# Two inner norms: the first two projections start with nine unnormalised tiles, and the third moves ahead of the barrier

## The chip, the cores and the metric

One core of one Trainium2 chip runs the whole program. The metric is the device time of one execution in microseconds (us), the median of several runs. The engines are TensorE (PE in the rows, its weight loads PEld), VectorE (DVE), ScalarE (ACT), GpSimd (POOL) and SyncE (SP), which issues the stream of weights.

## What is computed

Three layers of a sequence model on x of 512 positions by 2048 features, then a last norm. Each layer is a norm, one wide projection, a mixer and an output projection that is added to the residual:

```python
def rmsnorm(x, g):
    y = xf * lax.rsqrt(jnp.mean(xf * xf, axis=-1, keepdims=True) + EPS)
    return (y * g)
def even_layer(x, ...):
    hn = rmsnorm(x, norm_g)
    proj = hn @ w_in          # q, k, v, u, z_a, z_b
    ...
    return x + jnp.concatenate([o_a, o_b], axis=-1) @ w_out
def odd_layer(x, ...):
    hn = rmsnorm(x, norm_g)
    proj = hn @ w_in          # q, k, v, z, f_logit
    log_f = jax.nn.log_sigmoid(f_logit + b_forget)
    ...
    return x + o @ w_out
```

The factor of the norm, rsqrt(mean of the squares), belongs to a position; the gain g belongs to a feature. The change is about the norms ahead of `even_layer` and of `odd_layer`, called inner norms here. In the even layer u goes through a state-space model (S5), whose matrices are made on the chip out of small parameters; in the odd layer the sum over positions of log_f is subtracted from the attention scores.

## The kernel before, in words

**Tiles and split.** Features lie on the 128 partitions, positions (512) in the free dimension, so x is KT = 16 tiles of 128x512 in `mix`. All float32 products are made of three rounded ones: a value is split in a rounded part (`hi`) and what is left (`lo`), and hi·hi, lo·hi and hi·lo are summed in PSUM. One output tile of 128 features (`gemm`, L274) is 16 k-tiles of three matmuls, 48 in all. `gemm_two` (L297) does two output tiles together, k-tile by k-tile, 96 matmuls, as the operands come out of a norm.

**The weights.** A tile of weights comes in two halves of 512 KB. SyncE loads a half into one of two `raw` places (L267) once the half two before it is split. ScalarE makes its hi part (`cast`, L486, instruction at L495), which waits for the load and for TensorE to be done with the place in `w_hi`; GpSimd then makes the lo part (L2527) and reports it in `split_done`, for which TensorE waits. I call these two a cast and a rest. Casts stand by hand in ScalarE's program, in `taken` (L497) for instance: cast, read-out of the finished output tile, cast. GpSimd does the rests in the order of the stream.

**Output projection and norm.** In `out_tensor` (L347) TensorE makes 16 output tiles; VectorE adds the residual into `mix` (L363) and sums the squares (`accumulate`, L334) that ScalarE makes (L383). Behind the last one `norm_tensor` (L329) sums over the partitions by one matmul with ones (L332), ScalarE takes the root (L442), VectorE the reciprocal (`rstd`, L455). Then for each of 16 tiles: VectorE multiplies by gain and `rstd` (L459) into one of four buffers, ScalarE rounds (L450), VectorE subtracts (L466), and TensorE multiplies that k-tile into the first two projections (`gemm_two`, L308 to L310).

**Barrier.** `meet` (L243) drains TensorE, ScalarE and VectorE and lets each on when all three are there. GpSimd and SyncE take no part. One stands behind the first two projections at both inner norms.

**Even layer behind its barrier.** The first two projections are tiles N_U and N_U + 1 of u. ScalarE issues five loads of parameters (`s5_scalar`, L2094) and takes u tile by tile (`take_u`, L2102). VectorE (`s5_vector`, L2244) waits for those loads and runs a chain of 89 small instructions, then `make` (L2344). TensorE (`s5_tensor`, L2006) does the tiles N_U + 2 to N_U + 5 of u, then `form(0, 0)` (L2047: L2054 and L2061), which needs what `make` left, then the tiles N_U + 6 and N_U + 7.

**Odd layer behind its barrier.** The first two projections are the forget gates (tile N_F) and q of head 0 (N_ODD = N_F + 1). ScalarE (`forget_scalar`, L1919) and VectorE (`forget_vector`, L1934) turn the gates into a running sum in a chain, the result goes to memory and comes back (`load_decay`, L1630), and only then ScalarE takes q, k, v and z of head 0 (`take`). TensorE goes on with tile N_ODD + 1 (k), which waits for the read-out of the gates, then N_ODD + 2 (v), which waits for the read-out of q:

```python
            for j in range(at.heads, 4):
                gemm(pe, at.n0 + j, (at.n0 + j) % 2, free=(evac_act, at.n0 + j - 1 - at.shift))
```

## Time and profile before

| | us |
|---|---|
| median of 3 runs | 3190.93 (3188.35 to 3192.02) |
| the profiled execution, its own time | 3191.25 |
| its span, first to last instruction | 3189.4 |
| TensorE busy | 2995.7 (94% of the span) |
| VectorE, ScalarE, GpSimd busy | 1166.8, 1175.7, 1206.6 (37, 37, 38%) |
| granted clock of TensorE, mean | 0.975 |

The profile gives each engine's instructions in order of time, with the idle time before them in brackets and what ended it. TensorE is busy nearly throughout, so what counts are the few stretches in which it is not. A matmul's duration in a row overlaps the next one's; the distance of two starts is what it costs.

### The profile page before, as it was taken

The numbers are of one execution on the slowest core, as the hardware profiler recorded it, in microseconds if no ns is written. First come the engines' busy times: TensorE is split into PE (matmuls) and PEld (weight loads), VectorE is DVE, ScalarE is ACT, GpSimd is POOL, SyncE is SP. The second block draws the span as 40 slices with busy tenths as digits, with TensorE's granted clock in tenths as the row PEclk, the third lists the DMA queues.
The fourth block names the chain that finished last, engine by engine and source line by source line (L and its number), as shares of the span: only waits on it lengthen the run. The fifth ranks groups of instructions, "written<-read, shape, count | busy, mean of one in ns | idle before, by whom it ended". The sixth has DMA issues, their size and how long they took to land.

```text
span 3189.4 us, 47246 instructions
## 1 busy us (share of the span) xinstructions
PE 2995.7 (94%) x18318; PEld 2388.6 (75%) x18318; DVE 1166.8 (37%) x1684; ACT 1175.7 (37%) x1577; POOL 1206.6 (38%) x549
## 2 busy tenths in 40 slices
PE   6999998989998988999989987998999999999998
PEld 5777776767776877777766766886888888888786
DVE  4555555333443128578814334114111111111112
ACT  4333333235565223333324443223333333333322
POOL 3222220433325434566623322443333333333542
PEclk9999999999999999999999998999999999999999
DMA  4211110322212442222223222442222223222232
GB/s 155 96 55 55 55 61 21 96 69 80 79 62 68 161 132 82 84 96 92 96 97 106 79 79 86 148 139 80 93 91 89 92 89 92 92 86 91 90 125 99
DMA packets 95331, 290.25 MB, mean 91 GB/s; under 512 B 10048, under 2 KB 14432, under 8 KB 94704
## 3 DMA queue, kind: packets, MB, share of 16 engines
q1 hardware_dynamic: 64512, 233.14, 23.2%
q10 hardware_dynamic: 30704, 55.43, 5.1%
q8 instruction: 90, 1.47, 0.2%
q14 instruction: 25, 0.20, 0.0%
HBM read 265.40 MB, written 23.13 MB: 90 GB/s over the span
## 4 chain that ended last, share of the span: by engine, by line
PE 61%; issue 20%; DVE 8%; POOL 5%; PEld 3%; ACT 2%; DMA 1%; PEldq 1%; DVEq 0%; ACTq 0%; POOLq 0%; SPq 0%
PE ps L291 14%; PE ps L293 14%; PE ps L292 14%; POOL w_lo L2527 5%; PE ps L688 3%; PE ps L690 3%; PE ps L689 3%; DVE arena L2375 1%; DVE arena L2405 1%; PE ps L1539 1%; PE ps L1557 1%; DVE mix L2368 1%; PE ps L740 1%; DVE arena L2412 1%; PE ps L1754 1%
## 5 line engine op out<-in xcount | busy, mean ns | idle before, releaser
L2527 POOL TENSOR_TENSOR w_lo<-raw,w_hi 128x1024 fp32r<-128x1024 f32 x442 | 1069.9, 2423 | 1897.6 <-ACT w_hi L495 1896.4
L291 PE MATMUL ps<-act_hi,w_hi 128*128 128x512 f32 x2240 | 890.8, 398 | 33.9 <-POOL w_lo L2527 19.4
L293 PE MATMUL ps<-act_lo,w_hi 128*128 128x512 f32 x2240 | 877.0, 392 | 0.0
L292 PE MATMUL ps<-act_hi,w_lo 128*128 128x512 f32 x2240 | 876.7, 391 | 0.0
L495 ACT ACTIVATE w_hi<-raw 128x1024 fp32r<-128x1024 f32 x442 | 466.6, 1056 | 712.1 <-PE ps L293 339.7
L291 PEld LDWEIGHTS ps<-act_hi,w_hi 128*128 128x128 f32 x2240 | 423.9, 189 | 133.6 <-issue 42.0
L292 PEld LDWEIGHTS ps<-act_hi,w_lo 128*128 128x128 f32 x2240 | 424.3, 189 | 90.6 <-issue 4.3
L293 PEld LDWEIGHTS ps<-act_lo,w_hi 128*128 128x128 f32 x2240 | 423.5, 189 | 89.4
L688 PE MATMUL ps<-act_hi,w_hi 128*128 128x512 f32 x768 | 309.1, 403 | 13.7 <-ACT arena L780 13.7
L689 PE MATMUL ps<-act_hi,w_lo 128*128 128x512 f32 x768 | 300.2, 391 | 0.0
L690 PE MATMUL ps<-act_lo,w_hi 128*128 128x512 f32 x768 | 300.0, 391 | 0.0
L363 DVE TENSOR_TENSOR mix<-ps,arena 128x512 f32 (+1 forms) x48 | 33.2, 692 | 436.9 <-PE ps L293 403.3
L688 PEld LDWEIGHTS ps<-act_hi,w_hi 128*128 128x128 f32 x768 | 144.7, 188 | 49.4 <-issue 19.7
L690 PEld LDWEIGHTS ps<-act_lo,w_hi 128*128 128x128 f32 x768 | 144.6, 188 | 31.3
L689 PEld LDWEIGHTS ps<-act_hi,w_lo 128*128 128x128 f32 x768 | 144.9, 189 | 29.1 <-issue 1.4
L992 PE MATMUL ps<-act_hi,w_hi 128*128 128x512 f32 x352 | 154.9, 440 | 0.0
L1664 DVE TENSOR_TENSOR ps<-ps,arena 128x128 f32<-128x128 f32 (+1 forms) x64 | 27.1, 492 | 347.5 <-PE ps L1539 347.5
L994 PE MATMUL ps<-act_lo,w_hi 128*128 128x512 f32 x352 | 138.9, 394 | 0.0
L993 PE MATMUL ps<-act_hi,w_lo 128*128 128x512 f32 x352 | 138.2, 393 | 0.0
L1680 DVE TENSOR_TENSOR mix<-ps,arena 128x512 f32 (+1 forms) x16 | 11.1, 692 | 287.9 <-PE ps L1557 287.9
L383 ACT ACTIVATE arena<-mix 128x512 f32 (+1 forms) x48 | 30.3, 630 | 224.9 <-DVE mix L363 224.9
L308 PE MATMUL ps<-act_hi,w_hi 128*128 128x512 f32 x192 | 80.6, 420 | 31.6 <-DVE act_lo L466 15.7
(374 smaller groups left out, 3469.9 us busy)
## 6 DMA issues: line engine op xcount, KB each, us to landing
raw<-stream SPq DMA_DIRECT2D x442, 512.0 KB, 3.5
arena<-residual ACTq DMA_DIRECT2D x48, 256.0 KB, 2.7
residual<-mix ACTq DMA_DIRECT2D x32, 256.0 KB, 2.1
mix<-x ACTq DMA_DIRECT2D x4, 1024.0 KB, 9.7
residual<-arena ACTq DMA_DIRECT2D x4, 1024.0 KB, 6.9
kept_qk<-mix ACTq DMA_DIRECT2D x16, 256.0 KB, 2.1
arena<-kept_qk ACTq DMA_DIRECT2D x16, 256.0 KB, 3.7
arena<-decays ACTq DMA_DIRECT2D x16, 256.0 KB, 3.1
```

What stands on the lines that cost most here:

```text
L291: pe.matmul(dst, w_hi[:, slot, j, :], act_hi[:, kt, :], start=first, stop=False)
L292: pe.matmul(dst, w_lo[:, slot, j, :], act_hi[:, kt, :], start=False, stop=False)
L293: mm = pe.matmul(dst, w_hi[:, slot, j, :], act_lo[:, kt, :], start=False, stop=last)
L308: a = pe.matmul(dst, w_hi[:, slot, j, :], act_hi[:, kt, :], start=kt == 0, stop=False)
L495: nc.scalar.activation(w_hi[:, s, :, :], src[:, s % 2, :, :], ACT.Copy).then_inc(cast_done, 1)
L688: self.pe.matmul(dst, w_hi[:, slot, j, :], act_hi[:, kt, :], start=kt == 0, stop=False)
L689: self.pe.matmul(dst, w_lo[:, slot, j, :], act_hi[:, kt, :], start=False, stop=False)
L690: mm = self.pe.matmul(dst, w_hi[:, slot, j, :], act_lo[:, kt, :], start=False, stop=kt == KT - 1)
L992: pe.matmul(dst, w_hi[:, slot, kt % HK, :], act_hi[:, kt, :], start=kt == 0, stop=False)
L993: pe.matmul(dst, w_lo[:, slot, kt % HK, :], act_hi[:, kt, :], start=False, stop=False)
L994: mm = pe.matmul(dst, w_hi[:, slot, kt % HK, :], act_lo[:, kt, :], start=False, stop=kt == KT - 1)
L2527: nc.gpsimd.tensor_tensor(w_lo[:, s, :, :], src[:, s % 2, :, :], w_hi[:, s, :, :].bitcast(F32), ALU.subtract).then_inc(split_done, 1)
```

## The change

The norm's matmul leaves the end of `out_tensor` in the first two layers. As VectorE puts tiles 0 to 8 into `mix`, ScalarE rounds mix times gain, without the norm's factor (`plain_round`), and VectorE subtracts (`plain_rest`), into 18 places of their own. `first_tensor` takes the place of `gemm_two`: the k-tiles 0 to 8 of the first two projections from those, into PSUM banks 2 and 3, with the norm's matmul behind the fourth k-tile; then the k-tiles 9 to 15 with the norm's factor, as before, into banks 4 and 5. `first_vector` multiplies banks 2 and 3 by `rstd` and adds 4 and 5. The norm makes its 16 tiles in the order 9 to 15, 0 to 8, and ahead of the barrier TensorE does the third projection (N_U + 2, N_F + 2) out of them in the order of k. Four casts move from behind the barrier to places behind the tiles 4, 10, 12 and 14 of the norm's order, in `norm_scalar`. The loops over the norm's tiles and five pairs of output tiles are written out. The last norm keeps its form.

```diff
-                        pe.wait_ge(act_ready[0], act_ready[1] + kt + 1)
+                        place = kt if len(act_ready) == 2 else act_ready[2].index(kt)
+                        pe.wait_ge(act_ready[0], act_ready[1] + place + 1)
...
+        PLAIN = 9
+        NORM_ORDER = [*range(PLAIN, KT), *range(PLAIN)]
+        plain_hi = [slots(arena_r, j) for j in range(PLAIN)]
+        plain_lo = [slots(arena_r, j) for j in (9, 10, 11, 12, 13, 14, 15, 20, 28)]
+        first_out = [slots(arena, 24), slots(arena, 25)]
+        plain_rounded = sem("plain_rounded")
+        plain_split = sem("plain_split")
+        first_scaled = sem("first_scaled")
+        first_summed = sem("first_summed")
+
+        def first_tensor(pe, n, norm):
+
+            def products(bank, tile, kt, hi, lo, first, last):
+                dst, slot, j = ps[:, bank, :], 2 * (tile % 2) + kt // HK, kt % HK
+                a = pe.matmul(dst, w_hi[:, slot, j, :], hi, start=first, stop=False)
+                pe.matmul(dst, w_lo[:, slot, j, :], hi, start=False, stop=False)
+                return a, pe.matmul(dst, w_hi[:, slot, j, :], lo, start=False, stop=last)
+
+            pe.wait_ge(split_done, n * 2 + 3)
+            for kt in range(PLAIN):
+                if kt == HK:
+                    pe.wait_ge(split_done, n * 2 + 4)
+                pe.wait_ge(plain_split, PLAIN * (norm - 1) + kt + 1)
+                for tile in (n, n + 1):
+                    _, mm = products(2 + tile - n, tile, kt, plain_hi[kt], plain_lo[kt], kt == 0, kt == PLAIN - 1)
+                    if tile == n and kt == HK - 1:
+                        mm.then_inc(pe_half, 1)
+                if kt == 3:
+                    norm_tensor(pe, norm)
+            for kt in range(PLAIN, KT):
+                pe.wait_ge(norm_lo, KT * norm + (kt - PLAIN) + 1)
+                for tile in (n, n + 1):
+                    a, mm = products(4 + tile - n, tile, kt, act_hi[:, kt, :], act_lo[:, kt, :], kt == PLAIN,
+                                     kt == KT - 1)
+                    if kt == KT - 1:
+                        mm.then_inc(pe_half, 1)
+                    if tile > n and kt == KT - 1:
+                        a.then_inc(pe_half, 1)
+            gemm(pe, n + 2, n % 2, free=(evac_dve, KT * norm), act_ready=(norm_lo, KT * norm, NORM_ORDER))
+
+        def plain_round(act, norm, ft):
+            nc.scalar.activation(plain_hi[ft], mix_tile(ft), ACT.Copy, scale=gain(norm, ft)).then_inc(plain_rounded, 1)
+
+        def plain_rest(dve, norm, ft):
+            dve.wait_ge(plain_rounded, PLAIN * (norm - 1) + ft + 1)
+            nc.vector.scalar_tensor_tensor(
+                out=plain_lo[ft], in0=mix_tile(ft), scalar=gain(norm, ft), in1=plain_hi[ft].bitcast(F32),
+                op0=ALU.mult, op1=ALU.subtract).then_inc(plain_split, 1)
+
+        def first_vector(dve, n, norm):
+            dve.wait_ge(pe_half, 2 * (n + 2))
+            for j in range(2):
+                nc.vector.tensor_tensor(first_out[j], ps[:, 2 + j, :], rstd, ALU.mult).then_inc(first_scaled, 1)
+            for j in range(2):
+                dve.wait_ge(first_scaled, 2 * (norm - 1) + j + 1)
+                nc.vector.tensor_tensor(first_out[j], first_out[j], ps[:, 4 + j, :],
+                                        ALU.add).then_inc(first_summed, 1)
...
-            norm_tensor(pe, layer + 1)
+            if layer == 2:
+                norm_tensor(pe, layer + 1)
...
+                    if layer < 2 and isinstance(ft, int) and 0 <= ft + j - 1 < PLAIN:
+                        plain_rest(dve, layer + 1, ft + j - 1)
...
+                if not last_layer and isinstance(ft, int) and ft + j < PLAIN:
+                    plain_round(act, layer + 1, ft + j)
...
-            with act.Fori(0, KT // 4) as four:
-                ft = four * 4
-                for j in range(4):
-                    act.wait_ge(norm_t, ft + (KT * (norm - 1) + j + 1))
-                    nc.scalar.activation(act_hi[:, bass.ds(ft + j, 1), :].rearrange("p a t -> p (a t)"),
-                                         norm_in[j], ACT.Copy).then_inc(norm_hi, 1)
+            n = (0, N_U, N_F)[norm]
+            weights = {3: 0, 9: 1, 11: 2, 13: 3}
+            for i, ft in enumerate(NORM_ORDER):
+                act.wait_ge(norm_t, KT * (norm - 1) + i + 1)
+                nc.scalar.activation(act_hi[:, ft, :], norm_in[i % 4], ACT.Copy).then_inc(norm_hi, 1)
+                if i in weights:
+                    cast(act, n * 2 + 4 + weights[i], (2 * n + weights[i]) % 4)
...
+            def rest(i):
+                ft = NORM_ORDER[i]
+                dve.wait_ge(norm_hi, KT * norm + i + 1)
+                nc.vector.tensor_tensor(act_lo[:, ft, :], norm_in[i % 4], act_hi[:, ft, :].bitcast(F32),
+                                        ALU.subtract).then_inc(norm_lo, 1)
+
+            if norm < 3:
+                for i, ft in enumerate(NORM_ORDER):
+                    if i >= 2:
+                        rest(i - 2)
+                    if i >= 4:
+                        dve.wait_ge(norm_lo, KT * norm + i - 3)
+                    scaled(ft, i % 4)
+                for i in (KT - 2, KT - 1):
+                    rest(i)
+                first_vector(dve, (0, N_U, N_F)[norm], norm)
...
-            for j in range(at.heads, 4):
+            for j in range(at.heads + 1, 4):
...
+                if isinstance(u, int) and u == 0 and j == 0:
+                    act.wait_ge(first_summed, 4)
+                    nc.scalar.activation(at_q_in, first_out[1], ACT.Copy, scale=at.scale).then_inc(evac_act, 1)
+                    return
...
-            pe.wait_ge(evac_dve, 2 * KT)
-            gemm_two(pe, N_F, norm_lo, 2 * KT)
+            first_tensor(pe, N_F, 2)
 
         def forget_scalar(act):
             act.dma_start(at_cmask, consts[:, C_ODD:C_ODD + P]).then_inc(at_const, 16)
-            par = N_F % 2
-            cast(act, N_F * 2 + 4, (2 * par) % 4)
-            act.wait_ge(pe_half, N_F * 2 + 2)
-            nc.scalar.activation(fg_t[0], ps[0:FR, par, :], ACT.Identity,
+            act.wait_ge(first_summed, 3)
+            nc.scalar.activation(fg_t[0], first_out[0][0:FR, :], ACT.Identity,
                                  bias=prm[0:FR, PRM_BF:PRM_BF + 1]).then_inc(evac_act, 1)
-            cast(act, N_F * 2 + 5, (2 * par + 1) % 4)
...
-            pe.wait_ge(evac_dve, KT)
-            gemm_two(pe, N_U, norm_lo, KT)
+            first_tensor(pe, N_U, 1)
...
-            for n in range(N_U + 2, N_U + S5_TILES):
+            for n in range(N_U + 3, N_U + S5_TILES):
...
+                if j < 2:
+                    act.wait_ge(first_summed, j + 1)
+                    nc.scalar.activation(mix_tile(8 + j), first_out[j], ACT.Copy).then_inc(evac_act, 1)
+                    return
```

The first place where the order changes is ScalarE's program at the first inner norm. Before: behind the norm's root, the roundings (L450, here four of a loop of four passes), the barrier (`met`), the five loads of parameters, the first cast, the first read-out of u.

```order
L442 ACTIVATE arena<-ps,eps 128x512 [waits res_stored]
...
L450 ACTIVATE act_hi<-arena 128x512
...
L2096 DMA arena<-consts 128x512 [waits met]
L2098 DMA arena<-s_b 128x512 x2
L2100 DMA arena<-s_c 128x512 x2
L495 ACTIVATE w_hi<-raw 128x1024 [waits pe_half,raw_loaded0]
L2104 ACTIVATE mix<-ps 128x512 [waits pe_half]
```

Now (L518 is the rounding, L565 the cast, L2175 the read-out of u's first two tiles):

```order
L518 ACTIVATE act_hi<-arena 128x512 [waits norm_t] x4
L565 ACTIVATE w_hi<-raw 128x1024 [waits pe_half,raw_loaded0]
L518 ACTIVATE act_hi<-arena 128x512 [waits norm_t] x6
L565 ACTIVATE w_hi<-raw 128x1024 [waits pe_half,raw_loaded1]
L518 ACTIVATE act_hi<-arena 128x512 [waits norm_t] x2
L565 ACTIVATE w_hi<-raw 128x1024 [waits pe_half,raw_loaded0]
L518 ACTIVATE act_hi<-arena 128x512 [waits norm_t] x2
L565 ACTIVATE w_hi<-raw 128x1024 [waits pe_half,raw_loaded1]
L518 ACTIVATE act_hi<-arena 128x512 [waits norm_t] x2
L2165 DMA arena<-consts 128x512 [waits met]
L2167 DMA arena<-s_b 128x512 x2
L2169 DMA arena<-s_c 128x512 x2
L2175 ACTIVATE mix<-arena 128x512 [waits first_summed] x2
```

Four casts, and with them four rests on GpSimd, now stand among the roundings; none is left between the barrier and the two read-outs.

The second place is ScalarE's program behind the second inner norm's barrier, now: L1995 is the read-out of the gates, L2002 the store of the running sum, L1706 its load, L1659 the read-out of q, L1656 that of k.

```order
L1993 DMA arena<-consts 128x128 [waits met]
L1995 ACTIVATE arena<-arena,prm 16x512 [waits first_summed]
L1998 ACT_TABLE_LOAD
L1998 ACTIVATE arena<-arena 16x512 [waits fg]
L2000 ACT_TABLE_LOAD
L2000 ACTIVATE arena<-arena,eps 16x512 [waits fg]
L2002 DMA decays<-arena 16x512 [waits fg]
L1706 DMA arena<-decays 128x512 [waits decay_stored]
L1659 ACTIVATE arena<-arena 128x512 [waits first_summed]
L565 ACTIVATE w_hi<-raw 128x1024 [waits pe_half,raw_loaded0]
```

The casts that stood ahead of and behind the gates' read-out, and the one ahead of q's read-out, are gone from here; q is still read out behind the load of the running sum.

## Rows read from the trace of the kernel before

**Rows 1.** TensorE's timeline, first inner norm; columns: start us, us, engine, line, operation

```profile
1171.64 0.39 PE L292 MATMUL ps<-act_hi,w_lo 128*128 128x512 f32 x1
...
1183.43 0.39 PE L293 MATMUL ps<-act_lo,w_hi 128*128 128x512 f32 x1
...
1186.12 1.12 PE L332 MATMUL ps<-arena,ones 128*128 128x512 f32 x2 [2.30 <-DVE arena L343]
...
1195.10 0.76 PE L308 MATMUL ps<-act_hi,w_hi 128*128 128x512 f32 x1 [7.86 <-DVE act_lo L466]
...
1218.76 0.39 PE L310 MATMUL ps<-act_lo,w_hi 128*128 128x512 f32 x1
...
1225.24 0.76 PE L291 MATMUL ps<-act_hi,w_hi 128*128 128x512 f32 x1 [6.09 <-POOL w_lo L2527]
...
1230.33 0.39 PE L291 MATMUL ps<-act_hi,w_hi 128*128 128x512 f32 x1
```

**Rows 2.** VectorE's timeline in the same norm

```profile
1189.34 3.35 DVE L455 RECIPROCAL arena<-arena 128x512 f32<-128x512 f32 x1 [3.28 <-ACT arena L442]
...
1194.26 0.69 DVE L466 TENSOR_TENSOR act_lo<-arena,act_hi 128x512 fp32r<-128x512 f32 x1
...
1212.85 0.69 DVE L466 TENSOR_TENSOR act_lo<-arena,act_hi 128x512 fp32r<-128x512 f32 x1 [0.19 <-ACT act_hi L450]
```

**Rows 3.** GpSimd's timeline behind that norm

```profile
1222.75 4.67 POOL L2527 TENSOR_TENSOR w_lo<-raw,w_hi 128x1024 fp32r<-128x1024 f32 x2 [34.05 <-ACT w_hi L495]
...
1230.97 4.75 POOL L2527 TENSOR_TENSOR w_lo<-raw,w_hi 128x1024 fp32r<-128x1024 f32 x2 [3.56 <-ACT w_hi L495]
```

**Rows 4.** TensorE's waits from 1184 to 1350 us: total, times, longest

```profile
PE ps L2054 <- DVE arena L2375: 6.2, 1, 6.2
...
PE ps L2061 <- DVE arena L2375: 4.8, 2, 3.9
```

**Rows 5.** VectorE's preparation for the state-space stage, its timeline

```profile
1225.74 1.72 DVE L2253 TENSOR_SCALAR s_p<-prm 128x32 f32<-128x32 f32 x1 [12.19 <-DMA arena<-s_c]
1227.49 0.18 DVE L2254 TENSOR_SCALAR s_p<-s_p 128x32 f32<-128x32 f32 x1
...
1231.05 2.37 DVE L2269 TENSOR_TENSOR s_p<-prm,s_p 128x32 f32<-128x32 f32 x1
1233.45 2.30 DVE L2253 TENSOR_SCALAR s_p<-s_p 128x32 f32<-128x32 f32 x1
...
1281.30 2.03 DVE L2375 TENSOR_TENSOR arena<-mix 64x320 f32<-64x320 f32 x4
```

**Rows 6.** VectorE's timeline in the gated unit, two instructions of one line

```profile
1954.90 0.69 DVE L2483 TENSOR_TENSOR arena<-arena,mix 128x512 f32<-128x512 f32 x1 [1.29 <-ACT arena L2470]
...
1961.35 2.42 DVE L2483 TENSOR_TENSOR arena<-arena,mix 128x512 f32<-128x512 f32 x1 [5.03 <-ACT arena L2470]
```

**Rows 7.** GpSimd's timeline at the second of them

```profile
1960.82 2.40 POOL L2527 TENSOR_TENSOR w_lo<-raw,w_hi 128x1024 fp32r<-128x1024 f32 x1 [2.25 <-ACT w_hi L495]
```

**Rows 8.** TensorE's timeline around the second inner norm's barrier

```profile
2192.04 0.39 PE L310 MATMUL ps<-act_lo,w_hi 128*128 128x512 f32 x1
...
2196.58 0.77 PE L291 MATMUL ps<-act_hi,w_hi 128*128 128x512 f32 x1 [4.15 <-POOL w_lo L2527]
...
2209.93 0.47 PE L291 MATMUL ps<-act_hi,w_hi 128*128 128x512 f32 x1 [0.81 <-POOL w_lo L2527]
```

**Rows 9.** ScalarE's timeline behind the same barrier

```profile
2193.92 0.66 ACT L1924 ACTIVATE arena<-ps,prm 16x512 f32<-16x512 f32 x1
...
2206.26 1.06 ACT L495 ACTIVATE w_hi<-raw 128x1024 fp32r<-128x1024 f32 x1 [4.08 <-DMA decays<-arena]
2207.22 0.58 ACT L1583 ACTIVATE arena<-ps 128x512 f32<-128x512 f32 x1
```

**Rows 10.** VectorE's timeline there

```profile
2195.36 1.35 DVE L1940 TENSOR_SCALAR arena<-arena 16x512 f32<-16x512 f32 x1
2196.75 2.73 DVE L1942 SCALAR_TENSOR_TENSOR arena<-arena 16x512 f32<-16x512 f32 x1
```

More of the change, by code:

```diff
@@ L364, in pair @@
                                             ALU.add).then_inc(evac_dve, 1)
-                    if j or not isinstance(ft, int):
+                    if j or not (isinstance(ft, int) and ft == 0):
                         accumulate(dve, layer + 1, ft + (j - 1), 1 - j)
-            pair(0)
-            with dve.Fori(1, KT // 2) as two:
+                    if layer < 2 and isinstance(ft, int) and 0 <= ft + j - 1 < PLAIN:
+                        plain_rest(dve, layer + 1, ft + j - 1)
+            apart = 1 if layer == 2 else PLAIN // 2 + 1
+            for two in range(apart):
+                pair(two * 2)
+            with dve.Fori(apart, KT // 2) as two:
                 pair(two * 2)
@@ L399, in tile @@
                     cast(act, ft * 2 + (2 * (n0 + j + 2) + 1), (2 * (n0 + j) + 1) % 4)
-            for j in range(2):
-                tile(0, j)
-                res_load(act, 2 + j, j).then_inc(res_loaded[j], 16)
-            with act.Fori(1, KT // 2 - 1) as two:
+                if not last_layer and isinstance(ft, int) and ft + j < PLAIN:
+                    plain_round(act, layer + 1, ft + j)
+            apart = 1 if last_layer else PLAIN // 2 + 1
+            for ft in range(0, 2 * apart, 2):
+                for j in range(2):
+                    tile(ft, j)
+                    res_load(act, ft + 2 + j, j).then_inc(res_loaded[j], 16)
+            with act.Fori(apart, KT // 2 - 1) as two:
                 ft = two * 2
@@ L458, in scaled @@
             def scaled(ft, j):
-                nc.vector.scalar_tensor_tensor(
-                    out=norm_in[j], in0=mix_tile(ft + j), scalar=prm[:, bass.ds(ft + (PRM_G + KT * norm + j), 1)],
+                return nc.vector.scalar_tensor_tensor(
+                    out=norm_in[j], in0=mix_tile(ft), scalar=prm[:, bass.ds(ft + (PRM_G + KT * norm), 1)],
                     in1=rstd, op0=ALU.mult, op1=ALU.mult).then_inc(norm_t, 1)
-            def rest(ft, j):
-                dve.wait_ge(norm_hi, ft + (KT * norm + j + 1))
-                hi, lo = (t[:, bass.ds(ft + j, 1), :].rearrange("p a t -> p (a t)") for t in (act_hi, act_lo))
-                nc.vector.tensor_tensor(lo, norm_in[j % 4], hi.bitcast(F32), ALU.subtract).then_inc(norm_lo, 1)
@@ L468, in four_tiles @@
-            def four_tiles(ft, first=False):
-                for j in range(4):
-                    if norm == 3:
-                        if not first:
-                            dve.wait_ge(out_turned, ft + (j - 3))
-                    elif not (first and j < 2):
-                        rest(ft, j - 2)
-                        if not first:
-                            dve.wait_ge(norm_lo, ft + (KT * norm + j - 3))
-                    scaled(ft, j)
-            four_tiles(0, True)
-            with dve.Fori(1, KT // 4) as four:
-                four_tiles(four * 4)
@@ L482, in norm_vector @@
-            if norm < 3:
-                for j in (2, 3):
-                    rest(KT - 4, j)
+            def rest(i):
[14 more added lines that the diff above has]
+                return
@@ L486, in cast @@
+            for j in range(4):
+                scaled(j, j)
+            with dve.Fori(1, KT // 4) as four:
+                for j in range(4):
+                    dve.wait_ge(out_turned, four * 4 + (j - 3))
+                    scaled(four * 4 + j, j)
         def cast(act, m, s):
@@ L2103, in take_u @@
                 n = N_U + j
+                if j < 2:
+                    act.wait_ge(first_summed, j + 1)
+                    nc.scalar.activation(mix_tile(8 + j), first_out[j], ACT.Copy).then_inc(evac_act, 1)
+                    return
                 taken(act, n, n % 2, lambda: nc.scalar.activation(mix_tile(8 + j), ps[:, n % 2, :], ACT.Copy))
```

## Prediction

> **What bounds the kernel now.** The page gives TensorE 94% of the span, so I read TensorE's timeline where it has holes. At the first inner norm [rows 1] its last output matmul starts at 1183.43, the norm's matmul runs at 1186.12, and the first projection matmul comes at 1195.10 after 7.86 us of idle: those are the root, the reciprocal of 3.35 and the first scaled, rounded and split tile [rows 2]. The two projections then end at 1218.76 + 0.39 = 1219.15, the barrier follows, and the next matmul waits to 1225.24 for a GpSimd rest. The diff aims at these two holes, about 17 us at each of two norms.
>
> The next question is what the time behind the barrier hangs on. The summary of TensorE's waits [rows 4] shows two more, 6.2 and 3.9 us, at the matmuls of `form`, both for VectorE. Its timeline [rows 5] is one unbroken chain from 1225.74, when the five parameter loads issued behind the barrier have landed, to 1281.30 + 2.03 = 1283.33. TensorE passes `form` at 1283.33 + 1.1 = 1284.4, and work that reached it 10.1 us too early gained nothing. So in the even layer the time is the barrier's end plus 65.3 us, whatever TensorE does in between. In the odd layer TensorE waits little: 4.15 us and 0.81 us [rows 8]. But the matmul at 2209.93 (tile N_ODD + 2) is the one whose tile needs q read out, and q is read out at 2207.22 [rows 9], behind the forget chain.
>
> **The change, part by part.** Times are on the trace's own clock.
>
> (a) Nine plain k-tiles. Matmuls follow each other at (1183.43 − 1171.64) / 52 = 0.227 us [rows 1]. 54 of them take 12.2 us, and they start at once at 1183.66. The rounding and the split of each plain tile lie in the output stage, where ScalarE and VectorE are mostly idle (busy 37% each); I cost them at nothing, and if that cover failed they would be some 0.7 + 0.7 us a tile.
>
> (b) The norm's matmul now stands behind 24 plain ones: 1183.66 + 5.4 = 1189.1 instead of 1186.12, so the whole norm moves back by 3.0 us. TensorE finishes the plain tiles at 1196.8 or so (with some 0.9 of its 1.12 for the norm's matmul) and gets the first scaled tile at 1198.1. The hole of 11.3 us is down to about 1.
>
> (c) The norm's 16 tiles are VectorE's: 1194.26 to 1212.85 + 0.69 [rows 2], about 1.27 us a tile. TensorE needs 1.36 a tile while two projections share it, but the third projection alone needs only 0.68 a tile, and it wants k-tiles 0 to 8, which come last in the new order. With the 3.0 of (b) the last split ends at 1216.5. Nine k-tiles of the third projection wait for VectorE; the last eight k-tiles (24 matmuls, 5.4 us) stand behind the last split.
>
> (d) The four casts, and so four rests, now fall into the norm. Before, GpSimd had been idle for 34.05 us when it took them up at 1222.75 [rows 3]. What a rest does to VectorE is seen elsewhere: the same instruction of the same line, two operands in SBUF, takes 0.69 us alone and 2.42 us when it is started under a rest of 2.40 [rows 6, 7]; small instructions of 0.18 take 2.37 and 2.30 under the pair at 1230.97 [rows 3, 5]. Both of VectorE's operations in the norm read two operands of 128x512 in SBUF, and there VectorE never rests, so it loses the whole of each: 4 × 2.35 = 9.4 us. The bounds are 0 (the rests fall where VectorE waits anyway) and 9.4; I take 9.4, since all four casts stand behind a rounding in the middle of VectorE's unbroken row. The Trainium skill, page "SBUF — State Buffer", section "SBUF: two separate sides", says that a VectorE operation with two SBUF inputs and a GpSimd operation take a shared pair of ports in turn, each for its whole length; by that rule the four rests cost all of their length here, as the rows say, and if they shared bandwidth instead, the sum would be some 5 us smaller at each norm.
>
> (e) So the last split ends at 1216.5 + 9.4 = 1225.9, and the third projection at 1225.9 + 0.15 + 5.4 + 0.2 = 1231.7. `first_vector` needs four operations of 0.69 and is through at 1228.8. The barrier ends 12.5 us later than before (1219.15), in exchange for one more projection (10.9 us) done ahead of it.
>
> (f) Even layer. The chain starts 12.5 later. It gets shorter by the rests that no longer meet it: one cut 1.72 − 0.18 = 1.5, two cut 2.37 + 2.30 − 0.37 = 4.3 [rows 5], together 5.8 (the fourth lay ahead of the chain). The other eight before `form` stay. `form` comes 12.5 − 5.8 = **6.7 us later**. The projection gained on TensorE's side is spent waiting: with 10.9 less to do there and a chain 5.8 shorter, its wait at `form` goes from 10.1 to at most 15.2 us. What follows `form` is as before.
>
> (g) Odd layer. The barrier goes from 2192.04 + 0.39 = 2192.43 to 2204.9. From it to the end of q's read-out were 2207.22 + 0.58 − 2192.43 = 15.4 us. Gone from this are the cast ahead of q (2207.22 − 2206.26 = 1.0) [rows 9] and two stalls of VectorE under rests: 2.73 − 0.7 = 2.0, and 1.35 less some 0.35, 1.0 [rows 10]. The cast ahead of the gates I count at nothing, as VectorE also waits for the mask's load. That leaves 11.4, and tile N_ODD + 2 starts at 2216.3. It starts behind 11 us of idle: at 1225.24, after 6.09 of idle, twelve matmuls took 1230.33 − 1225.24 = 5.1 instead of 2.7 us [rows 1], most of them at 1.2 GHz instead of 2.4, so 2.3 are lost which at 2209.93 were not. Against 2209.93: 2216.3 + 2.3 − 2209.9 = **8.7 us later**.
>
> (h) The last norm only loses its separate branch: nothing.
>
> Sum: 6.7 + 8.7 = +15.4 us. The profiled execution took 3191.25 us (span 3189.4), 0.3 above the median of the runs, so 3191.25 + 15.4 − 0.3 = 3206.3; I say **3206 us**, 0.5% slower. An unknown on top is TensorE's clock in the third projection, which has holes of up to 2.8 us in a row; a hole of 0.81 kept it high and one of 4.15 didn't [rows 8]. Being nearer to the first in what separates them from 6.09, I take 0; the other end is 2.3 at each norm, 4.6 in all. Ends of this case: 3199 (one and a half rests of 2.35 less at each norm, 7.0) and 3214 (clock 4.6, one more rest's wait, 2.35).
>
> **The rivals.**
>
> *The rests do not hold VectorE up* (B). Then (d) is 0: the third projection ends at 1216.5 + 5.8 = 1222.3, the barrier moves by 3.1, `form` by 3.1 − 5.8 = −2.7 and the odd layer by 8.7 − 9.4 = −0.7: −3.4, **3187.5 us**, no change that can be measured. For it speaks that a rest can slip in where VectorE waits for ScalarE behind a cast; against it rows 5 and 6.
>
> *Faster: the chain behind the first barrier sheds more rests than three* (C). The place is VectorE's chain of 57.6 us. Eight rests still meet it at 2.1 us each. If TensorE, late behind the barrier, delays the casts of tiles N_U + 6 and N_U + 7 so that those four rests land behind the chain's end, the chain loses 4 × 2.1 = 8.4 us more; with B that makes −3.4 − 8.4 = −11.8, **3179 us**. It decides from the point where TensorE finishes tile N_U + 5 later than VectorE finishes `make`. Against it: by (f) TensorE is up to 15 us early there.
>
> *The norm stays as slow and the clock falls too* (D): (e) plus 4.6, and a late load of a weight half that blocks ScalarE's last roundings: over 3214 us. The half that the fourth cast takes can only be loaded once the second rest is done, which leaves the last two roundings little margin.
>
> That the change doesn't do what it says would be plain tiles that TensorE waits for; TensorE would then show holes among the first 54 matmuls. The order of the splits and nearly 11 us per output tile speak against it.
>
> **How the numbers follow.** Two kernels of this size can be told apart by 0.2%, 6.4 us: faster is under 3184.5, slower over 3197.3. My case 0.70, of which 0.02 lies under 3197.3; B 0.14; C 0.09, with a bit of 0.01 for other gains; D 0.04; partial stalls between B and mine 0.02. Faster 0.10, same 0.18, slower 0.72. The range holds 8 in 10 when it reaches from B's 3187 to my case's upper end, 3214; it leaves out C, D and half of B. My case's own range is 3199 to 3214. The likeliest case gives the number.
>
> **What would show it.** Right: at the first norm, TensorE without a hole from 1183 to about 1197; the norm's matmul 3 us later; VectorE's operations L459 and L466 as they are numbered then with four of some 3 us instead of 0.7; TensorE's waits in the third projection of some 10 us; the barrier at about 1232; the wait at `form` grown to some 15 us with the chain 52 us long; in the odd layer an idle stretch of 11 us behind the barrier. Wrong: a barrier before 1225 (B), the wait at `form` under 8 us (C), holes among the plain products, or VectorE's operations at 0.7 throughout while the time still grows.

## The result, and the profile after

The changed kernel takes 3205.89 us (median of 5 runs, 3205.12 to 3209.52) against 3190.93 us (5 runs beside it, 3187.87 to 3192.89): a ratio of 1.0052, 95% interval 1.0037 to 1.0067. It is slower by 15.0 us; the forecast said 15.4. Its profiled execution took 3205.12 us, with a span of 3203.3 against 3189.4: the two profiled executions lie 13.9 us apart.

TensorE's timeline at the first inner norm, which answers to [rows 1] (same columns; L391 is now the norm's matmul, L344 the products of the first two projections, L292 those of the third and of all later ones):

```profile
1188.29 1.02 PE L391 MATMUL ps<-arena,ones 128*128 128x512 f32 x2
...
1196.99 0.50 PE L344 MATMUL ps<-act_hi,w_hi 128*128 128x512 f32 x1 [0.83 <-DVE act_lo L535]
...
1213.88 0.50 PE L292 MATMUL ps<-act_hi,w_hi 128*128 128x512 f32 x1 [2.41 <-DVE act_lo L535]
...
1218.52 0.79 PE L292 MATMUL ps<-act_hi,w_hi 128*128 128x512 f32 x1 [2.02 <-DVE act_lo L535]
...
1223.16 0.79 PE L292 MATMUL ps<-act_hi,w_hi 128*128 128x512 f32 x1 [1.71 <-DVE act_lo L535]
...
1231.99 0.39 PE L294 MATMUL ps<-act_lo,w_hi 128*128 128x512 f32 x1
1236.03 0.77 PE L292 MATMUL ps<-act_hi,w_hi 128*128 128x512 f32 x1 [3.65 <-ACT mix L2175]
```

The hole of 11.3 us is gone: the norm's matmul stands among the plain products, and up to 1196.99 nothing is idle but 0.83 us. What is new are holes for VectorE's splits (6.7 us in the third projection and 2.3 in the first two), and the late end at 1231.99 + 0.39. VectorE's timeline in the same norm, which answers to [rows 2]:

```profile
1199.38 0.75 DVE L528 SCALAR_TENSOR_TENSOR arena<-mix,prm,arena 128x512 f32<-128x512 f32 x1
...
1200.65 2.88 DVE L528 SCALAR_TENSOR_TENSOR arena<-mix,prm,arena 128x512 f32<-128x512 f32 x1
...
1210.38 2.85 DVE L528 SCALAR_TENSOR_TENSOR arena<-mix,prm,arena 128x512 f32<-128x512 f32 x1
...
1215.02 2.85 DVE L528 SCALAR_TENSOR_TENSOR arena<-mix,prm,arena 128x512 f32<-128x512 f32 x1
...
1219.66 2.85 DVE L528 SCALAR_TENSOR_TENSOR arena<-mix,prm,arena 128x512 f32<-128x512 f32 x1
...
1223.81 1.28 DVE L382 TENSOR_TENSOR arena<-ps,arena 128x512 f32<-128x512 f32 x2
```

The row at 1199.38 is the usual scaling (L528), 0.75 us. Four others, 1200.65, 1210.38, 1215.02 and 1219.66, take 2.85 to 2.88. GpSimd's timeline, which answers to [rows 3], has a rest beginning just before each of them:

```profile
1200.56 2.41 POOL L2600 TENSOR_TENSOR w_lo<-raw,w_hi 128x1024 fp32r<-128x1024 f32 x1 [12.62 <-ACT w_hi L565]
1210.28 2.40 POOL L2600 TENSOR_TENSOR w_lo<-raw,w_hi 128x1024 fp32r<-128x1024 f32 x1 [7.31 <-ACT w_hi L565]
1214.92 2.40 POOL L2600 TENSOR_TENSOR w_lo<-raw,w_hi 128x1024 fp32r<-128x1024 f32 x1 [2.24 <-ACT w_hi L565]
1219.55 2.40 POOL L2600 TENSOR_TENSOR w_lo<-raw,w_hi 128x1024 fp32r<-128x1024 f32 x1 [2.24 <-ACT w_hi L565]
1250.47 4.68 POOL L2600 TENSOR_TENSOR w_lo<-raw,w_hi 128x1024 fp32r<-128x1024 f32 x2 [28.52 <-ACT w_hi L565]
```

The first two of the four operations behind the norm (L382 at 1223.81) have one operand in PSUM and take 0.64 us each. ScalarE's timeline gives the barrier, at the first of the five loads, and then the read-outs of u:

```profile
1232.46 0.34 ACTq L2165 DMA_DIRECT2D arena<-consts  x1
...
1234.79 1.15 ACT L2175 ACTIVATE mix<-arena 128x512 f32<-128x512 f32 x2 [11.62 <-issue]
```

Behind it, VectorE's chain, which answers to [rows 5]: what took 1.72, 2.37 and 2.30 there takes 0.18 or 0.19, as no rest runs from 1219.55 + 2.40 to 1250.47.

```profile
1238.87 0.18 DVE L2326 TENSOR_SCALAR s_p<-prm 128x32 f32<-128x32 f32 x1 [12.58 <-DMA arena<-s_c]
...
1242.64 0.19 DVE L2342 TENSOR_TENSOR s_p<-prm,s_p 128x32 f32<-128x32 f32 x1
```

TensorE's waits in this stretch (total, times, longest), which answer to [rows 4]; L2123 and L2130 are the matmuls of `form`:

```profile
PE ps L2130 <- DVE arena L2448: 6.8, 2, 5.9
PE ps L292 <- DVE act_lo L535: 6.7, 5, 2.4
PE ps L2123 <- DVE arena L2448: 5.9, 1, 5.9
PE ps L292 <- POOL w_lo L2600: 4.2, 1, 4.2
PE ps L292 <- ACT mix L2175: 3.6, 1, 3.6
```

In the odd layer TensorE's timeline, which answers to [rows 8], shows the barrier at 2209.75 + 0.39 and then the idle stretch of 11.29 us ahead of tile N_ODD + 2:

```profile
2209.75 0.39 PE L294 MATMUL ps<-act_lo,w_hi 128*128 128x512 f32 x1
2221.43 0.77 PE L292 MATMUL ps<-act_hi,w_hi 128*128 128x512 f32 x1 [11.29 <-ACT arena L1659]
...
2234.49 0.39 PE L292 MATMUL ps<-act_hi,w_hi 128*128 128x512 f32 x1
```

The 48 matmuls of that tile take 2234.49 − 2221.43 = 13.06 us; before, the next tile started 11.00 us behind the 2209.93 of [rows 8]:

```profile
2220.93 0.39 PE L291 MATMUL ps<-act_hi,w_hi 128*128 128x512 f32 x1
```

So the low clock behind the idle stretch costs 2.1 us here.

ScalarE's and VectorE's timelines there answer to [rows 9] and [rows 10]: the mask's load right at the barrier, q's read-out 10.5 us later, and the two steps that had stood under a rest at 0.42 and 0.68 us.

```profile
2210.22 0.34 ACTq L1993 DMA_DIRECT2D arena<-consts  x1
...
2220.70 0.63 ACT L1659 ACTIVATE arena<-arena 128x512 f32<-128x512 f32 x1 [4.01 <-DMA decays<-arena]
```

```profile
2212.86 0.42 DVE L2010 TENSOR_SCALAR arena<-arena 16x512 f32<-16x512 f32 x1
2213.31 0.68 DVE L2012 SCALAR_TENSOR_TENSOR arena<-arena 16x512 f32<-16x512 f32 x1
```

To compare traces I count from the last residual addition ahead of each norm (VectorE, L363 before, L423 after), which before starts at 1183.97 and 2157.65 and after at 1183.17 and 2163.56. The barrier's mark is the first load that ScalarE issues behind it (before 1219.23 and 2192.51, after 1232.46 and 2210.22):

| us from that addition | before | after | forecast |
|---|---|---|---|
| last split done, first norm | 29.6 | 40.7 | 42.0 |
| barrier, first norm | 35.3 | 49.3 | 47.8 |
| second part of `form` starts | 99.4 | 107.2 | 106.1 |
| barrier, second norm | 34.9 | 46.7 | 47.4 |
| tile N_ODD + 2 starts | 52.3 | 57.9 | 58.7 |

### The profile page after: what moved, and what is told of

It is laid out like the page before. It is cut to its first block, busy times and chain, and to the rows that moved or that the text cites. A ratio compares the mean times of both kernels' runs of the same rounds, so it can differ in the third digit from the quotient of the medians.

```text
span 3203.3 us, 46942 instructions
## 1 busy us (share of the span) xinstructions
PE 3003.2 (94%) x18318; PEld 2390.4 (75%) x18318; DVE 1193.6 (37%) x1710; ACT 1184.1 (37%) x1595; POOL 1207.9 (38%) x549
## 4 chain that ended last, share of the span: by engine, by line
PE 37%; issue 37%; POOL 12%; DVE 8%; PEld 2%; ACT 2%; DMA 1%; PEldq 0%; POOLq 0%; DVEq 0%; ACTq 0%; SPq 0%
POOL w_lo L2600 12%; PE ps L292 7%; PE ps L293 7%; PE ps L294 7%; PE ps L758 3%; PE ps L760 3%; PE ps L759 3%; DVE arena L2448 1%; DVE arena L2478 1%; PE ps L810 1%; DVE mix L2441 1%; DVE arena L528 1%; DVE arena L2485 1%; PE ps L1828 1%; PE ps L1819 1%
## 5 line engine op out<-in xcount | busy, mean ns | idle before, releaser
L292 PE MATMUL ps<-act_hi,w_hi 128*128 128x512 f32 x2240 | 895.2, 400 | 54.3 <-DVE act_lo L535 13.2
L565 ACT ACTIVATE w_hi<-raw 128x1024 fp32r<-128x1024 f32 x442 | 466.4, 1055 | 673.2 <-PE ps L294 348.8
L292 PEld LDWEIGHTS ps<-act_hi,w_hi 128*128 128x128 f32 x2240 | 425.3, 190 | 160.9 <-issue 50.4
L758 PE MATMUL ps<-act_hi,w_hi 128*128 128x512 f32 x768 | 309.0, 402 | 13.7 <-ACT arena L850 13.7
L423 DVE TENSOR_TENSOR mix<-ps,arena 128x512 f32 (+1 forms) x48 | 33.2, 692 | 419.3 <-PE ps L294 384.6
L758 PEld LDWEIGHTS ps<-act_hi,w_hi 128*128 128x128 f32 x768 | 144.6, 188 | 49.3 <-issue 19.8
L1062 PE MATMUL ps<-act_hi,w_hi 128*128 128x512 f32 x352 | 154.1, 438 | 0.0
L1754 DVE TENSOR_TENSOR mix<-ps,arena 128x512 f32 (+1 forms) x16 | 11.1, 692 | 288.5 <-PE ps L1627 288.5
L447 ACT ACTIVATE arena<-mix 128x512 f32<-128x512 f32 (+1 forms) x48 | 30.3, 631 | 224.6 <-DVE mix L423 224.6
L1062 PEld LDWEIGHTS ps<-act_hi,w_hi 128*128 128x128 f32 x352 | 66.0, 188 | 21.4 <-issue 7.6
```

What stands on the lines that cost most here:

```text
L292: pe.matmul(dst, w_hi[:, slot, j, :], act_hi[:, kt, :], start=first, stop=False)
L423: nc.vector.tensor_tensor(mix_tile(ft + j), ps[:, (n0 + j) % 2, :], res_in[j], ALU.add).then_inc(evac_dve, 1)
L565: nc.scalar.activation(w_hi[:, s, :, :], src[:, s % 2, :, :], ACT.Copy).then_inc(cast_done, 1)
L758: self.pe.matmul(dst, w_hi[:, slot, j, :], act_hi[:, kt, :], start=kt == 0, stop=False)
L1062: pe.matmul(dst, w_hi[:, slot, kt % HK, :], act_hi[:, kt, :], start=kt == 0, stop=False)
```

## The experiments

The theory: (1) the time of either layer is the barrier's end plus a chain of VectorE and ScalarE that starts there; (2) the barrier is late because the third projection needs all 16 scaled tiles and because four rests take 2.1 us each from VectorE in the norm. Each kernel stands beside the kernel before on the same chip, which took 3192.9 to 3193.4 us there. The changed kernel was run again on one of these chips, beside three of the kernels below (the kernel before and the changed one with both shortenings, and the latter with late casts); where a kernel is said to be so much under the changed one, its distance from the kernel before is set against 15.3 us. That run: 

> The changed kernel itself, beside which the others of this call stand. Expected as measured: 14 to 16 us over the kernel before.

 Measured 3208.20 us against 3192.90, ratio 1.005 (1.0036 to 1.0063), 15.3 us more.

**The plain tiles alone.** The third projection and its casts go back behind the barrier.

```diff
-            gemm(pe, n + 2, n % 2, free=(evac_dve, KT * norm), act_ready=(norm_lo, KT * norm, NORM_ORDER))
...
-            weights = {3: 0, 9: 1, 11: 2, 13: 3}
+            weights = {}
...
-            for j in range(at.heads + 1, 4):
+            for j in range(at.heads, 4):
...
-            for n in range(N_U + 3, N_U + S5_TILES):
+            for n in range(N_U + 2, N_U + S5_TILES):
```

> Edit: the changed kernel with its nine plain tiles, but the third projection and the four casts back behind the barrier. My theory (the time hangs on the barrier's end plus VectorE's and ScalarE's chains; the loss is the later barrier, made by the third projection and the rests inside the norm): no rest falls in the norm, the last split ends near 1216 us of the trace, the two sums that follow end near 1218.6, where the barrier was before (1219.15, with this trace 0.8 us ahead), so about 3191 us, within 3 of the kernel before. Rival 1 (the plain parts themselves cost, by their work in the output stage and the written-out loops): slower than before by 5 us or more. Rival 2 (TensorE's holes are the time): the hole of 11 us is gone at both norms, 3172 to 3180 us.

Measured 3190.81 us against 3193.43, ratio 0.9993 (0.9984 to 1.0002): no change that the interval can tell from nothing. TensorE has no hole of 11 us in the norm any more, and nothing is won. VectorE's timeline, last residual addition and last of the two sums, and ScalarE's, the barrier:

```profile
1187.96 0.69 DVE L422 TENSOR_TENSOR mix<-ps,arena 128x512 f32 x1 [9.60 <-PE ps L294]
...
1221.34 1.27 DVE L384 TENSOR_TENSOR arena<-arena,ps 128x512 f32<-128x512 f32 x2
```

```profile
1222.70 0.34 ACTq L2169 DMA_DIRECT2D arena<-consts  x1
```

1222.70 − 1187.96 = 34.7 us against 35.3 before. TensorE's waits show where the hole went: into one of 17.1 us behind the barrier.

```profile
PE ps L292 <- POOL w_lo L2606: 17.1, 1, 17.1
```

So the plain tiles cost nothing and bring nothing; both rivals fall. The whole loss is in the third projection and its casts.

**The rests in the norm, taken away.** GpSimd's four rests of each norm shrink to 128x8 elements; the rest of the lo part of those weights is left out, so this kernel does less work than it should. (For this the loop over the rests is written out where the four stand.)

```diff
+                if isinstance(m, int) and (2 * (N_U + 2) <= m < 2 * (N_U + 4) or 2 * (N_F + 2) <= m < 2 * (N_F + 4)):
+                    nc.gpsimd.tensor_tensor(w_lo[:, s, 0, 0:8], src[:, s % 2, 0, 0:8],
+                                            w_hi[:, s, 0, 0:8].bitcast(F32), ALU.subtract).then_inc(split_done, 1)
+                    return
```

> Edit: the changed kernel, with GpSimd's four rests in each norm cut to 128x8 elements; the lo part of those four halves of weights is left out. My theory (each full rest holds VectorE up for its length, 2.1 to 2.35 us): VectorE's operations under a rest go from about 2.85 us back to 0.75, the barrier comes 8.5 to 9.5 us earlier at both norms, and the time falls by 17 to 20 us, to 3186 to 3189 us. Rival (the rests only happen to run beside VectorE, the barrier is late because TensorE and VectorE have more work ahead of it): under 4 us of change, 3202 to 3206 us.

Measured 3188.68 us, ratio 0.9986 (0.9977 to 0.9995), 4.8 under the kernel before and so some 20 under the changed one. VectorE's timeline, a scaling from the middle of the norm, and the last two sums:

```profile
1204.08 0.74 DVE L528 SCALAR_TENSOR_TENSOR arena<-mix,prm,arena 128x512 f32<-128x512 f32 x1
...
1221.25 1.28 DVE L385 TENSOR_TENSOR arena<-arena,ps 128x512 f32<-128x512 f32 x2
```

Behind the reciprocal no operation of the norm takes over 0.75 us; the last split comes 32.3 us after the residual addition instead of 40.7, 8.5 us earlier, which is four times 2.1. The barrier comes 38.2 us after it at both norms, instead of 49.3 and 46.7: at the first norm 2.6 us more than the stalls, because there the last projection had also run at the low clock in part (see the last section). 11.1 and 8.5 make 19.6 of the some 20. The rival falls.

**The same without leaving work out.** The third and fourth cast move behind the norm's last rounding.

```diff
-            weights = {3: 0, 9: 1, 11: 2, 13: 3}
+            weights = {3: 0, 9: 1}
...
+            for j in (2, 3):
+                cast(act, n * 2 + 4 + j, (2 * n + j) % 4)
```

> Edit: the changed kernel, with nothing but the third and fourth cast moved behind the norm's last rounding; all work is done. My theory (two of the four stalls go): 7 to 10 us under the changed kernel, which stood 15.3 over the kernel before: 5 to 8 us over it. Rival (the stalls come back in the two sums or at the barrier): under 3 us of gain.

Measured 3198.92 us against 3193.27, ratio 1.0016 (1.0008 to 1.0025): 5.7 us over the kernel before, 9.6 less than the changed kernel's 15.3. The rival falls. GpSimd's and VectorE's timelines: the second rest still stops a scaling (2.85), the third and fourth (one row, x2) begin at 1221.93 beside the sums (L382, 0.64 each), and the scaling at 1218.24 takes 0.74.

```profile
1212.24 2.39 POOL L2602 TENSOR_TENSOR w_lo<-raw,w_hi 128x1024 fp32r<-128x1024 f32 x1 [7.30 <-ACT w_hi L567]
1221.93 4.75 POOL L2602 TENSOR_TENSOR w_lo<-raw,w_hi 128x1024 fp32r<-128x1024 f32 x2 [7.30 <-ACT w_hi L567]
```

```profile
1212.34 2.85 DVE L530 SCALAR_TENSOR_TENSOR arena<-mix,prm,arena 128x512 f32<-128x512 f32 x1
...
1218.24 0.74 DVE L530 SCALAR_TENSOR_TENSOR arena<-mix,prm,arena 128x512 f32<-128x512 f32 x1
...
1221.55 1.28 DVE L382 TENSOR_TENSOR arena<-ps,arena 128x512 f32<-128x512 f32 x2
```

The last split comes 4.2 us earlier at both norms (36.5 instead of 40.7), and the barrier 6.9 and 4.2 earlier (42.4 at both); the 2.7 more at the first norm is again the clock. Some of it comes back: the loads issued behind the barriers land 0.8 and 1.6 us later than in the changed kernel. What makes them late was not tried.

**The chain behind the first barrier.** The first 45 steps of `s5_vector` read only `prm` and their own scratch. They move behind the first pair of output tiles of layer 0, and the wait for the five loads to the first step that reads them.

```diff
             for two in range(apart):
                 pair(two * 2)
+                if layer == 0 and two == 0:
+                    s5_prepare(dve)
...
-            dve.wait_ge(s5_loaded, 16 * 5)
...
+            dve.wait_ge(s5_loaded, 16 * 5)
             for dst, src, f in zip(s5_t, (br, bi, bi, br), (s5_cr, s5_ci, s5_cr, s5_ci)):
```

> Edit: the changed kernel, with the first 45 steps of VectorE's preparation for the state-space stage, which read only parameters that are there from the start, behind the first pair of output tiles of layer 0, where VectorE is idle; the wait for the five loads moves to the first step that reads them. My theory (the even layer's time is the barrier plus that chain): form comes about 11 us earlier and the time falls by 9 to 12 us, to 3194 to 3197 us. Rival (TensorE is the limit, its waits at form are only moved): under 2 us.

Measured 3199.31 us, ratio 1.0015 (1.0006 to 1.0024): 5.9 over the kernel before, some 9 under the changed one; the rival falls. The gain is at the low end of the 9 to 12 expected, the time itself above the 3194 to 3197. The second part of `form` starts 96.6 us after the residual addition instead of 107.2. TensorE's waits from 1180 to 1340 us (L2132 is `form`'s second part):

```profile
PE ps L2132 <- DVE arena L2459: 6.9, 1, 6.9
```

The wait of 4.2 us for a rest is gone too, and `form` as a whole still waits 8.0 us (with 1.1 at its first part).

**The read-out of q.**

```diff
                 if isinstance(u, int) and u == 0 and j == 0:
-                    act.wait_ge(first_summed, 4)
-                    nc.scalar.activation(at_q_in, first_out[1], ACT.Copy, scale=at.scale).then_inc(evac_act, 1)
                     return
...
             nc.scalar.activation(fg_t[0], first_out[0][0:FR, :], ACT.Identity,
                                  bias=prm[0:FR, PRM_BF:PRM_BF + 1]).then_inc(evac_act, 1)
+            act.wait_ge(first_summed, 4)
+            nc.scalar.activation(slots(arena, 0), first_out[1], ACT.Copy, scale=odd.scale).then_inc(evac_act, 1)
             fg.wait(act, "n", 0)
```

> Edit: the changed kernel, with q of head 0 read out right behind the gates instead of behind the load of the running sum. My theory (tile N_ODD + 2 hangs on that read-out): TensorE's idle stretch of 11.3 us behind the second barrier shrinks to about 2, the next tile's rest is ready just in time, and the time falls by 8 to 10 us, to 3196 to 3198 us. Rival (the forget chain is needed by something else just behind, the scores of head 0 or the casts): the wait comes back there, and under 3 us are gained.

Measured 3198.16 us, ratio 1.0014 (1.0005 to 1.0023): 4.7 over the kernel before, 10.6 under the changed one; the rival falls. TensorE's waits in the odd layer, where one of 11.3 had stood:

```profile
PE ps L292 <- ACT arena L1996: 1.8, 1, 1.8
PE ps L292 <- POOL w_lo L2600: 1.3, 1, 1.3
```

**Both shortenings in both kernels.** If (1) is right, the kernel before must gain by them as well.

> Edit: the kernel before with both shortenings of the two chains (the first 45 preparation steps in the output stage; q of head 0 read out ahead of the forget chain). My theory: in the even layer TensorE's waits of 10 us at form go down to a few, in the odd layer only the 0.8 us go: 8 to 12 us faster than before, about 3183 us where before is 3193. Rival (the chains only matter in the changed kernel): within 3 us of before.

Measured 3178.94 us against 3192.90, ratio 0.9959 (0.9946 to 0.9973): 14.0 us less, where 8 to 12 were expected; the rival falls. TensorE's waits: the 10.1 us at `form` are gone (what is left at L2065 is a wait of 0.9 at a later use, which the kernel before has too, the second of the two of L2061 in [rows 4]), and the two holes of the norm stand as before.

```profile
PE ps L308 <- DVE act_lo L468: 7.9, 1, 7.9
PE ps L291 <- POOL w_lo L2540: 6.1, 1, 6.1
...
PE ps L2065 <- DVE arena L2388: 0.9, 1, 0.9
```

From one norm's last residual addition to the other's it is 960.0 us against 973.7, so 13.7 of the 14.0 are the even layer's: the preparation moved ahead. That leaves next to nothing for the read-out of q in the kernel before, while it is worth 10.6 in the changed kernel. The 3.6 us beyond the waits of 10.1 are for the most part the clock: without the idle time ahead of `form`, the first nine matmuls behind it take 2.2 us instead of 3.9, and its first part 1.0 instead of 2.0.

> Edit: the changed kernel with the same two shortenings. My theory: the two gains of 9 and 10 us add up, about 19 us under the changed kernel, 4 us under the kernel before, and no better than the kernel before with the same shortenings, because the rests still hold up the norm. Rival 1 (with the chains off the path the projections done ahead of the barrier pay): 5 us or more faster than the kernel before with both shortenings. Rival 2 (the gains overlap): less than 14 us under the changed kernel.

Measured 3185.19 us, ratio 0.9979 (0.997 to 0.9988): 7.7 under the kernel before where 4 was expected, 23 under the changed kernel where 19 was expected, and 6 over the kernel before with the same edits. Its runs are spread wider than those of the others, 3180.7 to 3189.5. Both rivals fall: the gains add up, 9.4 + 10.6 = 20.0, and where the other 3 come from was not tried. The further kernels build on this one.

> Edit: the previous kernel, with the third and fourth cast behind the norm's last rounding, so that two of the four rests fall beside the two sums, which read PSUM, and the barrier. My theory: VectorE loses two stalls of 2.1 us less in each norm, 4.2 us each, so 7 to 10 us under the previous kernel. Rival (the stalls only move to the sums behind the norm, or the casts hold ScalarE at the barrier): under 3 us.

Measured 3177.33 us, ratio 0.9952 (0.9939 to 0.9966): 15.6 under the kernel before, 7.9 less than without the late casts, as expected.

> Edit: the kernel with the plain tiles and the third projection behind the barrier (the first experiment), with both chains shortened. My theory: as the first experiment equals the kernel before, this one equals the kernel before with both shortenings, 14 us under the kernel before, within 3 us. Rival (the plain tiles pay once the chains are short): 5 us or more under that.

Measured 3178.44 us against 3193.27, ratio 0.9957 (0.9944 to 0.9969), 14.8 less: the same as the kernel before with both shortenings; the rival, that the plain tiles pay once the chains are short, falls.

**One stall more.** The first projection's eight plain k-tiles of its first half come first, and the first cast stands ahead of the norm's root.

```diff
-            weights = {3: 0, 9: 1}
+            weights = {9: 1}
...
+            if norm < 3:
+                n = (0, N_U, N_F)[norm]
+                cast(act, n * 2 + 4, (2 * n) % 4)
             act.wait_ge(norm_mm, norm)
```

> Edit: the kernel with both shortenings and the late third and fourth cast; in addition the first projection's eight plain k-tiles of its first weight half run ahead of the second projection's, so that this half is free before the norm's root, and the first cast stands there: its rest then falls beside the root and the reciprocal, where VectorE has no operation with two operands in SBUF. My theory: one stall of 2.1 us less in each norm, 3 to 5 us under that kernel (some 16 under the kernel before, it had 15.6), about 20 us under the kernel before. Rival (TensorE, not VectorE, then sets the norm's end, or the cast delays the root): within 1.5 us.

Measured 3176.02 us against 3193.27, ratio 0.995 (0.9937 to 0.9963): 17.3 less, 1.7 better than the kernel without it, which the intervals can't tell from nothing. The expectation of 3 to 5 failed; the rival's 1.5 is nearer. The stall did go: the barriers come 40.6 us after the residual additions instead of 42.4. But in the even layer the chain behind the barrier took 0.6 us more, and in the odd layer TensorE's next wait grew from 1.2 to 2.7:

```profile
PE ps L292 <- POOL w_lo L2619: 2.7, 1, 2.7
```

This and the late casts with both shortenings are the fastest kernels here; whether they beat the kernel before with both shortenings (ratios 0.995 and 0.9952 against 0.9959) is inside the intervals.

## Why the prediction was right

The direction, the two mechanisms and the sum hold. By its own steps:

- (a), (b): plain tiles at no cost and the norm 3.0 us later. The plain products start at once, the norm's matmul comes about 3 us later, and the first experiment shows that the cover holds: same time as before.
- (c), (d): the last split 12.4 us later by the sum, 11.2 measured. The four stalls are 2.1 us each (2.85 − 0.75), 8.5 in all, where I took 2.35 each, 0.9 too much at each norm: a rest runs for 2.4, but it had begun 0.1 us before the operation that it stops. The other 0.2 is not explained. The waits in the third projection came to 6.7 us, not to some 10. That rests hold VectorE up at all was shown by taking them away (−20 us) and by moving two of them (−9.6 us). The bound of 0 and with it rival B are refuted.
- (e): the barrier 12.5 us later by the sum. At the second norm it was 11.8, at the first 14.0. The difference of 2.2 is the clock (2.6), less 0.4 by which the kernel before was itself later at its first barrier. The clock is the unknown that I set to 0, and the reason I gave for the 0 doesn't carry: in length, a hole of 2.8 is nearer to the one of 4.15 behind which the clock was low (1.35 away) than to the one of 0.81 that kept it high (2.0 away). The windows of TensorE in the changed kernel (busy us of PE, PEld, DVE, ACT, POOL, then granted clock, DMA share, GB/s) show its last stretch ahead of the barrier at the first norm, and then at the second:

```profile
1224.00:1232.00 8.00, 8.00 (x26) 6.30 (x25) 2.28 (x4) 0.00 (x0) 0.00 (x0) 0.68 0.11 42
```

```profile
2204.00:2210.00 6.00, 6.00 (x27) 4.51 (x25) 2.67 (x5) 0.00 (x0) 0.00 (x0) 1.00 0.20 76
```

- (f): chain 5.8 us shorter; it was 6.2 (from the barrier's mark to `form`: 99.4 − 35.3 = 64.1 before, 107.2 − 49.3 = 57.9 after). `form` came 7.8 us later instead of 6.7. Some of that came back behind it: from one norm's last residual addition to the other's it was 980.4 us against 973.7, 6.7 more. Six matmuls at the low clock behind `form` instead of eight are 0.5 us of the 1.1; the rest is not explained, and that the layer's difference meets the forecast's 6.7 to the tenth is luck. The wait at `form` grew to 11.8 and not to 15, since TensorE first waited 3.6 us for u's read-outs and 4.2 for a rest behind ScalarE's sines; from the barrier on it waited 19.7 us in all, against 16.2 before (6.1 + 6.2 + 3.9).
- (g): 8.7 us later by the sum. Measured 5.6 by the start of tile N_ODD + 2, and 2.1 (not 2.3) for its start at the low clock, 7.7. The stretch from the barrier to that tile was 11.2 against my 11.4.
- The rivals: C needed rests to fall behind the chain's end, and all eight ran ahead of it. D's clock cost time at one norm of two; its other half, a late load that blocks the last roundings, did not come: ScalarE's roundings wait for VectorE's scalings alone. D needed over 3214.

The measured parts, 6.7 + 7.7, are 14.4; the measured difference is 15.0, in the second comparison 15.3. The profiled pair differs by 13.9, in part because the changed kernel came to the first norm 0.8 us earlier. The forecast of 15.4 is closer than its terms: the stalls were taken 0.9 too long at each norm, and the clock, set to 0, cost 2.6 at one. That these two nearly cancel is luck; the mechanism does not depend on it.

The stated upper end of 3214 is by its own terms 3206.3 + 4.6 + 2.35 = 3213.3.

## What to carry to other kernels

A hole on the busiest engine is worth what the chain that ends last goes through, not its length: here 11 us of TensorE's idle time at each norm went without a gain that can be told from nothing (ratio 0.9984 to 1.0002), since chains of VectorE and ScalarE start at the barrier behind it. Before moving work ahead of a barrier, ask what starts at the barrier. And a subtraction on GpSimd set beside VectorE operations with two operands in SBUF is paid nearly in full on VectorE (2.1 of its 2.4 us): put it where VectorE is idle or reads PSUM. The rests do not only stop operations with two operands in SBUF: in [rows 5] a small one with a single one (TENSOR_SCALAR, s_p<-s_p) takes 2.30 us under a rest instead of 0.18. The cheap edits were the ones on the chains: 14 us for the kernel before, nearly all of it by starting a part of VectorE's chain ahead of the barrier. No kernel with the plain tiles or the early third projection beats that one by more than the intervals allow.

## What was not expected of the hardware

TensorE's clock didn't cost the same in two stretches that are alike. It fell at both norms of the changed kernel, between holes of 0.3 to 2.4 us, and none as long as 4.15. But at the second norm it fell earlier, and was back for the last 27 matmuls ahead of the barrier; at the first it fell later (the matmul at 1215.15 still takes 0.51) and stayed low through the first 13 of those 27. A matmul behind a hole takes 0.79 or 0.80 us at the low level and 0.50 at the full one; the ones that follow each other take 0.63 and 0.39. First norm, then second:

```profile
1215.15 0.51 PE L292 MATMUL ps<-act_hi,w_hi 128*128 128x512 f32 x1 [0.30 <-DVE act_lo L535]
...
1229.24 0.40 PE L294 MATMUL ps<-act_lo,w_hi 128*128 128x512 f32 x1
```

```profile
2195.55 0.79 PE L292 MATMUL ps<-act_hi,w_hi 128*128 128x512 f32 x1 [0.30 <-DVE act_lo L535]
...
2203.55 0.50 PE L292 MATMUL ps<-act_hi,w_hi 128*128 128x512 f32 x1 [1.71 <-DVE act_lo L535]
```

The rerun of the changed kernel and the kernels with one shortening show the same: low at the end of the first norm's third projection (0.67 in the rerun), full in the second's. In the profiled execution of the changed kernel with both shortenings the first norm is like the second (1.00). It is 2.6 to 2.7 us at the barrier: 49.3 to 49.4 us from the residual addition in the four, 46.6 in the fifth and at every second norm (46.6 or 46.7). What decides where the clock falls was not tried.
